# Spreading a norm's root over a bank by transposes, with the root in nine steps in place of twelve

## The reference, cut to what matters

```python
def rms_norm(x, g):
    xf = x.astype(jnp.float32)
    y = xf * lax.rsqrt(jnp.mean(xf * xf, axis=-1, keepdims=True) + EPS)
    return (y * g.astype(jnp.float32)).astype(x.dtype)
```

## Time and profile before

| | us |
|---|---|
| median of 3 runs | 1990.87 (1989.4 to 1992.05) |
| the profiled execution, its time | 1990.34 |
| its span in the trace | 1988.6 |
| TensorE busy | 1951.0 (98%) |
| VectorE busy | 1195.8 (60%) |
| GpSimd busy | 1113.9 (56%) |
| ScalarE busy | 924.6 (46%) |

### The profile page before, as it was taken

The page is one execution under the profiler, slowest core; times in us unless marked ns, Lnnn a source line. Parts: engine busy times, 40 slices in busy tenths (PEclk is TensorE's granted clock), DMA queues, the critical chain, the costliest instruction groups (busy, mean ns, idle before and its releaser), DMA issues.

```text
span 1988.6 us, 25389 instructions
## 1 busy us (share of the span) xinstructions
PE 1951.0 (98%) x9308; PEld 1602.0 (81%) x9308; DVE 1195.8 (60%) x2004; ACT 924.6 (46%) x1740; POOL 1113.9 (56%) x847
## 2 busy tenths in 40 slices
PE   8999999999999999999999999999999999999997
PEld 6877887888888877878788888888777888888886
DVE  6773324353433488877676646856688775745855
ACT  5653336433333356545353433445477543443443
POOL 5344545454444456454566665755784576666652
PEclk9999999999999999999999999999999999999998
DMA  4122233232232321111323222223110322222221
GB/s 159 64 70 95 96 106 128 85 111 101 96 113 91 122 82 64 53 59 59 128 95 105 96 97 95 96 89 109 64 54 33 128 96 105 96 85 98 103 96 53
DMA packets 52107, 182.73 MB, mean 92 GB/s; under 512 B 5776, under 2 KB 6160, under 8 KB 51984
## 3 DMA queue, kind: packets, MB, share of 16 engines
q1 hardware_dynamic: 51984, 181.12, 26.0%
HBM read 174.80 MB, written 6.29 MB: 91 GB/s over the span
## 4 chain that ended last, share of the span: by engine, by line
PE 95%; DVE 3%; ACT 1%; issue 0%; DMA 0%; POOL 0%; SPq 0%; DVEq 0%; POOLq 0%
PE b L394 29%; PE b L396 28%; PE b L395 28%; PE b L416 3%; PE b L408 2%; PE b L449 1%; PE b L459 1%; PE b L440 1%; PE b L409 1%; PE b L439 1%; PE b L410 1%; PE b L427 0%; PE b L429 0%; PE b L428 0%; DMA raw<-in_w_first 0%
## 5 line engine op out<-in xcount | busy, mean ns | idle before, releaser
L240 POOL TENSOR_TENSOR ra<-raw,ra 128x512 fp32r<-128x512 f32 x632 | 881.0, 1401 | 781.7 <-ACT ra L284 779.1
L394 PE MATMUL b<-ra 128*128 128x512 f32 x2528 | 1001.9, 396 | 20.3 <-POOL ra L240 9.6
L396 PE MATMUL b<-ra 128*128 128x512 f32 x2528 | 986.6, 390 | 0.0
L395 PE MATMUL b<-ra 128*128 128x512 f32 x2528 | 985.8, 390 | 0.0
L284 ACT ACTIVATE ra<-raw 128x512 fp32r<-128x512 f32 x632 | 392.6, 628 | 536.4 <-PE b L396 529.9
L394 PEld LDWEIGHTS b<-ra 128*128 128x128 f32 x2528 | 475.8, 188 | 126.6 <-issue 17.1
L396 PEld LDWEIGHTS b<-ra 128*128 128x128 f32 x2528 | 475.4, 188 | 101.2
L395 PEld LDWEIGHTS b<-ra 128*128 128x128 f32 x2528 | 476.1, 188 | 93.2
L732 DVE TENSOR_TENSOR h<-b,h 128x512 f32<-128x512 f32 x136 | 91.7, 683 | 60.3 <-PE b L396 59.6
L623 DVE TENSOR_TENSOR tmp<-b,rb 128x512 f32<-128x512 f32 x64 | 43.9, 690 | 126.2 <-PE b L396 126.1
L616 DVE TENSOR_TENSOR ra<-b,ra 128x512 fp32r<-128x512 f32 (+4 forms) x166 | 91.7, 567 | 18.1 <-ACT ra L335 15.4
(11 more groups left out here) (277 smaller groups left out, 1929.8 us busy)
## 6 DMA issues: line engine op xcount, KB each, us to landing
raw<-in_f_g SPq DMA_DIRECT2D x40, 512.0 KB, 3.5
raw<-in_f_v SPq DMA_DIRECT2D x40, 512.0 KB, 3.5
raw<-in_f_d SPq DMA_DIRECT2D x40, 512.0 KB, 3.4
raw<-in_w_up SPq DMA_DIRECT2D x32, 512.0 KB, 3.5
raw<-in_w_down SPq DMA_DIRECT2D x32, 512.0 KB, 3.5
raw<-in_p_g SPq DMA_DIRECT2D x16, 512.0 KB, 3.5
raw<-in_w_gp SPq DMA_DIRECT2D x8, 512.0 KB, 3.5
raw<-in_w_ga SPq DMA_DIRECT2D x8, 512.0 KB, 3.5
```

Of the source, the lines that this page charges most:

```text
L240: e.tensor_tensor(wl, src, wh.bitcast(F), ALU.subtract).then_inc(*w_low.mark(n))
L394: e.matmul(ps, wh[:, c:c + 128], xh, start=start, stop=False)
L395: e.matmul(ps, wh[:, c:c + 128], xl, start=False, stop=False)
L396: last = e.matmul(ps, wl[:, c:c + 128], xh, start=False, stop=stop)
```

## The change

The spread uses TensorE's `transpose` in place of a product with the identity, on the same operands. The root takes nine instructions in place of twelve: the first estimate is one instruction (the bits of x times -0.5 plus a constant), then comes one round of four instructions of a higher order and one Newton round of three with changed constants. A second column block of `sm` (col + 4 to col + 8) holds u; the tile `smi` goes. The planner is told 2.1 us for the root.

```diff
@@ -456,9 +455,8 @@
             for q in range(4):
-                x = e.matmul(m.banks[STB][:, 128 * q:128 * q + 128],
-                             m.sm[:, col + q:col + q + 1].to_broadcast([128, 128]), m.ident[:, :],
-                             start=True, stop=True)
+                x = e.transpose(m.banks[STB][:, 128 * q:128 * q + 128],
+                                m.sm[:, col + q:col + q + 1].to_broadcast([128, 128]), m.ident[:, :])
             x.then_inc(*stat.mark(n))
@@ -497,7 +495,7 @@
-            x, y, s = banks[STB][:, 16:20], m.sm[:, col:col + 4], banks[STB][:, 32:36]
+            x, y, s, u = banks[STB][:, 16:20], m.sm[:, col:col + 4], banks[STB][:, 32:36], m.sm[:, col + 4:col + 8]
@@ -508,21 +506,28 @@
             w.wait_ge(stat, (n, 0))
-            e.tensor_scalar(m.smi[:, :], x.bitcast(I32), 1, None, ALU.arith_shift_right).then_inc(*stat.mark((n, 1)))
+            e.tensor_scalar(y.bitcast(I32), x.bitcast(I32), -0.5, float(0x5F3759DF), ALU.mult,
+                            ALU.add).then_inc(*stat.mark((n, 1)))
             w.wait_ge(stat, (n, 1))
-            e.tensor_scalar(y.bitcast(I32), m.smi[:, :], -1.0, float(0x5F3759DF), ALU.mult,
-                            ALU.add).then_inc(*stat.mark((n, 2)))
-            k = 2
-            for _ in range(3):
-                w.wait_ge(stat, (n, k))
-                e.tensor_tensor(s, x, y, ALU.mult).then_inc(*stat.mark((n, k + 1)))
-                w.wait_ge(stat, (n, k + 1))
-                e.scalar_tensor_tensor(out=s, in0=s, scalar=-0.5, in1=y, op0=ALU.mult,
-                                       op1=ALU.mult).then_inc(*stat.mark((n, k + 2)))
-                w.wait_ge(stat, (n, k + 2))
-                e.scalar_tensor_tensor(out=y, in0=s, scalar=1.5, in1=y, op0=ALU.add,
-                                       op1=ALU.mult).then_inc(*stat.mark((n, k + 3)))
-                k += 3
+            e.tensor_tensor(s, x, y, ALU.mult).then_inc(*stat.mark((n, 2)))
+            w.wait_ge(stat, (n, 2))
+            e.tensor_tensor(u, s, y, ALU.mult).then_inc(*stat.mark((n, 3)))
+            w.wait_ge(stat, (n, 3))
+            e.scalar_tensor_tensor(out=s, in0=u, scalar=-10.0 / 3.0, in1=u, op0=ALU.add,
+                                   op1=ALU.mult).then_inc(*stat.mark((n, 4)))
+            w.wait_ge(stat, (n, 4))
+            e.scalar_tensor_tensor(out=y, in0=s, scalar=5.0, in1=y, op0=ALU.add,
+                                   op1=ALU.mult).then_inc(*stat.mark((n, 5)))
+            w.wait_ge(stat, (n, 5))
+            e.tensor_tensor(s, x, y, ALU.mult).then_inc(*stat.mark((n, 6)))
+            w.wait_ge(stat, (n, 6))
+            e.scalar_tensor_tensor(out=s, in0=s, scalar=-27.0 / 1024.0, in1=y, op0=ALU.mult,
+                                   op1=ALU.mult).then_inc(*stat.mark((n, 7)))
+            w.wait_ge(stat, (n, 7))
+            e.scalar_tensor_tensor(out=y, in0=s, scalar=0.5625, in1=y, op0=ALU.add,
+                                   op1=ALU.mult).then_inc(*stat.mark((n, 8)))
             stat.at[n] = stat.n
@@ -798,7 +803,7 @@
     if kind == "columns":
-        return 2.8
+        return 2.1
```

More of the change, by code:

```diff
@@ L158, in __init__ @@
         self.sm = sb("sm", [128, 96], F)
-        self.smi = sb("smi", [128, 4], I32)
         self.gbuf = sb("gbuf", [128, 4, S], F)
```

## The result

The changed kernel takes 1978.69 us (median of 4 runs, 1977.87 to 1979.44) against 1991.46 for the kernel before (4 runs, 1989.4 to 1993.43): the ratio is 0.9933, 95% interval 0.9922 to 0.9945. The forecast of 1979.2 lies 0.5 us off. The profiled execution took 1979.44 us (its span is 1977.6), 10.9 us less than the profiled execution before.

A forecast was written before the change was run, and what follows sets the result against it. TensorE, busy 1951.0 of 1988.6 us, was taken to bound the kernel. Spread 8.3, tail 1.5 and moves 1.9 sum to 11.7 us less; against the median 1990.87 the forecast is 1979.2 us, range 1974.5 to 1985.

The forecast's parts named there:

- The spread, 8.3 us: TensorE at 18 norms inside the stream: transposes take 0.35 us in place of 0.81, saving 0.46 each, 8.3 us.
- The root in mid-kernel, 0: VectorE's shorter root inside the stream: worth nothing by itself, as other TensorE work lies between column sums and spread.
- The tail, 1.5 us: Last norm, where nothing covers: 0.6 us from the shorter root plus 0.9 from the last spread at half clock.
- The moves, 1.9 us: Earlier spreads shorten TensorE's pauses behind the second, fourth and fifth norms: 0.7 + 0.7 + 0.5 us.
- lower end: Of the moves at three norms: 0 gained, because another late instruction takes over the gap.
- The clock: Half-clock stretch of TensorE behind a pause: costs about 1.7 us, and one can come or go with the gaps.
- Rival (e): Slower by the clock: each of 18 spreads could bring a half-clock stretch of 1.7 us, 2009.8 us; chance 0.01.
- (a): Another layout changes TensorE's idle time: 1974 us if better, chance 0.10; 1984 if worse, chance 0.09.
- (c): Transpose of the repeated column is built as two passes like the product, 152 records, 1988.4 us; chance 0.02.
- (d): New layout brings long gaps with half-clock stretches, 4.1 us each, in the differential attention; four leave 1995.6; chance 0.03.
- (b): Saved spread passes come back as waiting because the feeders on GpSimd and VectorE set the pace, 1987.5 us; chance 0.05.

The follow-up runs named there:

- e3: Kernel before with only the planner's duration of a root set to 2.1 us in place of 2.8; 1990.36 us, ratio 0.9996.
- e9: Changed kernel with the twelve-step root of before, transposes and the planner's 2.1 kept; 1980.32 us, ratio 0.9945.
- e1: Kernel before with only the spread done by transposes, twelve-step root and the planner's 2.8 kept; 1981.42 us, ratio 0.9953.
- e4: Changed kernel with the planner's 2.8 us of before, transposes and nine-step root kept; 1977.72 us, ratio 0.9932.
- e5: Changed kernel with every transpose of a spread issued twice into the same place; 1985.93 us, ratio to before 0.9976.

## Why the prediction was right, and where its terms were off

Read from before to after by way of e3 and e9, net: the planner 0.5, the transposes 6.2, the root 2.4, the tail 1.6; together 10.7 us where the prediction added up 11.7. The shares hang on the order in which the parts are put in: in the order of before the transposes give 6.9 (e1), and the planner's number gives 1.35 on top of the other two (e4). The profiled pair differs by 10.9: one half-clock stretch less, but a start 0.4 us later and the pause at 45.

- **The spread, 8.3 us.** The price was right: 0.46 us a norm, 76 records, 0.35 us to the next product. That the turned operand is one column read over and over did not matter. The count was off: it lies bare, that is, shortens its piece, at 14 of 18 norms (6.2 us; 14 x 0.46 would be 6.4). At the four others VectorE ended last. The step that failed is the one that took 8.3 "because TensorE's waits are so few"; a piece can be on VectorE's chain with TensorE busy for 27.97 of 28.39 us. The Trainium skill ("TensorE: Matmul & The Clock Gate", section Terms) has four times for FP32. The trace does not agree: the measured groups are 0.81 and 0.35 us, 2.3 times, and the sum by the rows was the nearer one.
- **The root in mid-kernel, 0.** This failed: "inside the stream this is worth nothing by itself". The reason given, other work of TensorE between columns and spread, is true of the spread's own wait: the spread starts 2.96 us behind the root's end there (836.56 against 833.60). But the root also stands in VectorE's queue ahead of the softmax steps whose result TensorE wants next. That is worth 4 x 0.62 = 2.5 us in the changed order. In the order of before the root is worth 0.5 alone and 0.8 beside the transposes (e1 against e4). That these two misses, 2.1 too much for the spread and 2.4 too little for the root, nearly cancel in the sum is luck.
- **The tail, 1.5 us.** Measured 1.58: 0.61 for the root, 0.97 for the spread at half clock. (8 x 0.20 + 0.16 makes 1.76 and not 1.77; the root measured 1.77.)
- **The moves, 1.9 us.** Alone they gave 0.5, by e3. At the second norm the pause fell by 0.53 of the 0.68. At the fifth it fell from 0.99 to 0.44, as forecast:

```profile
736.02 0.51 PE L407 MATMUL b<-ra 64*128 64x512 f32 x2 [0.44 <-DVE ra L483]
```

  But that is lost again behind it: from the fifth to the fourteenth norm, with the heads laid out anew, e3 takes 263.25 us and the kernel before 263.3. At the fourth the pause did not fall, and the piece from there to the fifth norm takes 31.49 us in e4, with the planner's number of before, and in the changed kernel's second profile alike. ScalarE's timeline of the changed kernel behind that spread:

```profile
693.61 0.60 ACT L351 ACTIVATE tmp<-b 128x512 f32<-128x512 f32 x1 [1.23 <-PE b L395]
694.10 0.68 ACT L296 ACTIVATE ra<-b,vec 128x512 fp32r<-128x512 f32 x1
```

and of the kernel before:

```profile
696.18 0.60 ACT L352 ACTIVATE tmp<-b 128x512 f32<-128x512 f32 x1 [1.67 <-DVE b L686]
```

  VectorE's first product behind the spread, before:

```profile
695.48 0.70 DVE L686 TENSOR_TENSOR b<-fa,b 128x512 f32<-128x512 f32 x1 [2.75 <-PE b L459]
```

and now:

```profile
692.22 0.70 DVE L691 TENSOR_TENSOR b<-fa,b 128x512 f32<-128x512 f32 x1 [2.23 <-PE b L458]
```

  In the kernel before, ScalarE's first copy behind the end of the spread waits for that product and begins 0.70 us behind its start. Now the first copy there waits for a result of TensorE and begins at 693.61, 1.39 us behind VectorE's start. The 0.69 us in between is what the move had won, and the end of the pause keeps its new distance: 6.49 us behind VectorE's start in place of 5.80. So the lower end, "another late instruction takes over the gap", was the right value there. Which instruction takes it over is the reading of two traces; that copy was not moved by itself.
- **The clock.** 1.7 us was named for one stretch, 1.5 to 1.6 measured. It was kept out of the sum, and the medians show that it mattered (below). Rival (e) falls: with 76 transposes in the spreads, and 152 in e5, half clock appears inside the stream only at the three places where it appears without them. The rule of the Trainium skill ("TensorE: Matmul & The Clock Gate", Part 4), that the full clock does not engage for transposes, does not show here, where they stand among other matmuls: the granted clock is 1.00 over 694 to 994.
- **The rivals.** (a) falls: the new order alone moved the heads' section, from the fifth norm to the thirteenth, by only 0.3 us (225.5 in e3, 225.8 before). (c) falls with 76 records; (d) with 294.48 us busy in 694 to 994. (b) holds in a small part: at four norms of eighteen the saved passes did come back as waiting. The 400.00 us that were set against it are TensorE's; GpSimd is busy for 249.55 there.

The difference of the medians (12.8 us in the first comparison) is larger than the 10.7 because the executions of before carried more half-clock stretches: two and three in its profiles, one and none in those of the changed kernel. The mean granted clock says the same of the other runs; what in the program brings the stretches is open, as said. So the forecast of the median came within 0.5 us partly by luck: its sum was 1.0 us too large, and what it left out, the stretches above all, added about 1.5 us to the gain (1990.87 less 1978.69 is 12.2).

## What to carry to other kernels

An engine that is 98% busy can still hold pieces in which another engine's chain ends last; split the program at a repeating step, compare the piece lengths of two traces, and ask of each saved instruction whether the piece shrinks by its price. Work that is taken off an engine's stream can help what stands behind it there (0.62 us at each of four norms here), so "its result isn't needed yet" is no reason to cost it at nothing. And before a difference of one or two microseconds is put down to a change, look in the second profile of the same kernel for what comes and goes by itself.

## What was not expected of the hardware

- The half-clock stretch behind a pause is not a function of the pause's length. Behind 2.40 to 2.43 us near 700, TensorE was granted 0.50 in one execution of the kernel before and 1.00 in the other; a pause of 1.57 us near 1530 was followed by one in the first profile of the changed kernel and by none in the second. Behind the pause of 1.03 us at 138 none was seen in any profile.
- The one step of the root that works on SBUF alone is still uneven in mid-kernel. The new one, by records (ns min/median/max):

```profile
L518 DVE SCALAR_TENSOR_TENSOR b<-sm x19: 170/172/1053, 27.3 to 1967.2; 128x4 f32<-128x4 f32 x19
```

  Its longest value, 1053, is like that of the step that went (1025), though the median fell from 407 to 172. The steps behind the first one that touch a PSUM bank take 160 to 171 ns at all 19 norms.
- The pause of 0.9 us near 45 (TensorE's scores behind a sum of VectorE) is in one profile of before and of the changed kernel each and not in the other.
